# A fused attention, gMLP and expert layer: the key columns of two heads in one product, and the head products in other places

## The reference, cut

```python
q = (c_q @ w_uq).reshape(b, s, 8, 64 + 32)      # c_q: 256 wide, normalised; 32 columns get rope
k_nope = (c_kv @ w_uk).reshape(b, s, 8, 64)     # c_kv: 128 wide, normalised
v = (c_kv @ w_uv).reshape(b, s, 8, 64)
sc = (q_nope . k_nope + q_rope . k_rope) * 96 ** -0.5
sc = where(key_chunk <= q_chunk, sc, -max)      # chunks of 64 tokens
o = softmax(sc) @ v
```

## Time and profile before

| | |
|---|---|
| median of 3 runs | 1146.53 us (1145.36 to 1147.4) |
| profiled execution, span from first to last instruction | 1149.4 us |
| PE busy | 1098.1 us, 96% |
| DVE, ACT, POOL busy | 727.0, 562.0, 378.4 us |
| attention | about 97 to 265 us of the span |
| mean granted TensorE clock | 0.988 |

### The profile page before, as it was taken

One profiled execution on the slowest core, in us unless ns is written; L12 is line 12 of the kernel. 1 busy time (PEld: TensorE's weight loads), 2 busy tenths in 40 slices (PEclk: granted clock), 3 DMA queues, 4 the chain that ended last, 5 costly groups with the idle time before them and its releaser, 6 DMA issues.

```text
span 1149.4 us, 16228 instructions
## 1 busy us (share of the span) xinstructions
PE 1098.1 (96%) x5621; PEld 911.5 (79%) x5621; DVE 727.0 (63%) x939; ACT 562.0 (49%) x740; POOL 378.4 (33%) x270
## 2 busy tenths in 40 slices
PE   4999999999999999999999999979999999999986
PEld 4887888878887888888888788867888888877782
DVE  7877788874066621222223555579999988988847
ACT  6236677673164200000003222248888888878833
POOL 1403222224322233232330000115666666644410
PEclk9999999999999999999999999989999999999998
DMA  8010000022103111211203443569999999999737
GB/s 256 11 30 6 12 7 11 3 74 74 37 1 102 38 51 41 55 42 51 55 2 111 133 138 119 201 233 379 381 390 377 371 357 345 346 364 354 289 137 319
DMA packets 108858, 181.08 MB, mean 158 GB/s; under 512 B 32385, under 2 KB 69761, under 8 KB 108801
## 3 DMA queue, kind: packets, MB, share of 16 engines
q1 hardware_dynamic: 98432, 163.51, 41.4%
q0 software_dynamic: 10368, 16.80, 4.0%
HBM read 174.50 MB, written 26.74 MB: 175 GB/s over the span
## 4 chain that ended last, share of the span: by engine, by line
PE 74%; SPq 9%; DVE 8%; DMA 3%; issue 3%; ACT 2%; POOL 0%; POOLq 0%; ACTq 0%; DVEq 0%
PE ps L399 21%; PE ps L401 20%; PE ps L400 20%; SPq L536 6%; PE ps L765 3%; PE ps L727 2%; DMA raw_e<-in_w_exp_up_dram 2%; PE ps L1012 2%; SPq L532 1%; PE ps L941 1%; DVE negm L1524 1%; DVE pt_lo L1557 1%; DVE we_lo L1860 1%; PE ps L1087 1%; DMA yin<-y_dram 1%
## 5 line engine op out<-in xcount | busy, mean ns | idle before, releaser
L1860 DVE TENSOR_TENSOR we_lo<-raw_e,we_hi 128x2048 fp32r<-128x2048 f32 x105 | 239.7, 2284 | 34.9 <-ACT we_hi L1338 34.7
L1338 ACT ACTIVATE we_hi<-raw_e 128x2048 fp32r<-128x2048 f32 x105 | 200.6, 1912 | 16.5 <-DMA raw_e<-in_w_exp_up_dram 8.6
L399 PE MATMUL ps<-ht_hi,w_hi 128*128 128x512 f32 x432 | 170.1, 394 | 0.7 <-DVE ht_lo L1442 0.4
L401 PE MATMUL ps<-ht_hi,w_lo 128*128 128x512 f32 x432 | 168.3, 390 | 0.0
L400 PE MATMUL ps<-ht_lo,w_hi 128*128 128x512 f32 x432 | 168.2, 389 | 0.0
L393 POOL CAST w_hi<-raw 128x1024 fp32r<-128x1024 f32 x35 | 38.3, 1095 | 275.2 <-PE ps L401 202.2
L1686 DVE TENSOR_TENSOR mix<-ps,mix 128x512 f32<-128x512 f32 x16 | 11.0, 690 | 173.6 <-PE ps L401 173.6
L399 PE MATMUL ps<-we_hi,xst_hi 128*128 128x512 f32 x280 | 115.8, 413 | 0.4 <-DVE xst_lo L1864 0.4
L401 PE MATMUL ps<-we_hi,xst_lo 128*128 128x512 f32 x280 | 110.3, 394 | 0.0
L400 PE MATMUL ps<-we_lo,xst_hi 128*128 128x512 f32 x280 | 109.2, 390 | 0.0
L399 PEld LDWEIGHTS ps<-ht_hi,w_hi 128*128 128x128 f32 x432 | 81.3, 188 | 17.7 <-POOL w_lo L394 0.8
(11 more groups left out here) (311 smaller groups left out, 2518.0 us busy)
## 6 DMA issues: line engine op xcount, KB each, us to landing
raw_e<-in_w_exp_gate_dram SPq DMA_DIRECT2D x70, 512.0 KB, 6.6
raw_e<-in_w_exp_up_dram SPq DMA_DIRECT2D x70, 512.0 KB, 16.2
raw_e<-in_w_exp_down_dram SPq DMA_DIRECT2D x70, 512.0 KB, 8.6
raw<-in_w_in_dram SPq DMA_DIRECT2D x27, 512.0 KB, 3.9
yin<-y_dram SPq DMA_DIRECT2D x16, 512.0 KB, 10.0
xin<-in_x_dram SPq DMA_DIRECT2D x8, 512.0 KB, 8.1
xre<-in_x_dram SPq DMA_DIRECT2D x8, 512.0 KB, 5.3
h_dram<-h SPq DMA_DIRECT2D x8, 512.0 KB, 2.9
```

The lines of the kernel that those rows point to most:

```text
L399: pe.matmul(dst, st[0], mv[0], start=first, stop=False)
L401: return pe.matmul(dst, st[1], mv[0], start=False, stop=last)
L1338: act.activation(we_hi[c % 4][:, :], raw_e[c % NS][:, :], ACT.Copy).then_inc(sem("w_hi_ready"), 1)
L1860: dve.tensor_tensor(we_lo[c % NS][:, :], raw_e[c % NS][:, :], we_hi[c % 4][:, :].bitcast(F32), ALU.subtract).then_inc(sem("w_lo_ready"), 1)
```

## The change

Four things change, and waits and counts with them.

1. The key columns of heads 2m and 2m+1 are one stationary operand of 128 columns. Jobs 1 and 3 exist only for even heads (and are issued while an odd head is worked on); each fills 128 rows of bank 7, and ACT and DVE take each half into the `k_hi` and `k_lo` of its head: two copies and two subtractions per job.
2. `spread_sums` transposes to 64 partitions: the stationary operand has 64 columns, not 128.
3. Job 2 moves from the end of n=4 to the end of n=1. ACT's copy of it moves from n=5 to n=2. Job 1 moves from n=1 to n=4 of odd heads: on PE ahead of the transposes, on ACT behind `probs_high(4)` and ahead of `outputs(2h)`, on DVE behind `probs_low(4)` and ahead of `halves_added(2h)`. On ACT the copies of job 3 stand ahead of the exponential of n=7.
4. Even heads load 384 columns of weights, odd ones 256.

```diff
+        def jobs_of(h):
+            return (0, 2) if h % 2 else (0, 2, 1, 3) if h else (0, 1, 2, 3)
...
+        def keys_at(h, c):
+            return 4 * (h // 2) + 2 * c + h % 2 + 1
...
-                    elif j == 1:
-                        pe.wait_ge(sem("q_tmp_ready"), 2 * h + j // 2 + 1)
-                    elif j == 0 or h < 2 and j == 2:
-                        pe.wait_ge(sem("kv_lo_ready"), 2 * h + j // 2)
+                    elif j == 2:
+                        pe.wait_ge(sem("q_tmp_ready"), 2 * h + 1)
+                    elif j == 0 and h % 2:
+                        pe.wait_ge(sem("kv_lo_ready"), keys_at(h, 1))
                     else:
-                        pe.wait_ge(sem("o_ready"), 2 * (h - 1) + j // 3)
+                        pe.wait_ge(sem("o_ready"), 2 * h - (3, 2, 0, 1)[j])
...
-                        mm = mm3(pe, ps[0:NOPE, b, :], (hh[:, 256:320], hl[:, 256:320]),
+                        mm = mm3(pe, ps[:, b, :], (hh[:, 256:384], hl[:, 256:384]),
                                  (c_hi[:, 0, cs], c_lo[:, 0, cs]), True, True)
...
-                        mm = pe.transpose(ps[:, 7, i * P:(i + 1) * P],
-                                          rl[:, 4 * g + i:4 * g + i + 1].to_broadcast([P, P]), ident[:, :])
+                        mm = pe.transpose(ps[0:VH, 7, i * P:(i + 1) * P],
+                                          rl[:, 4 * g + i:4 * g + i + 1].to_broadcast([P, VH]), ident[:, :])
...
+                        if n == 4 and h % 2 and ahead:
+                            job(h + 1, 1)
                         prob_transposes(h, n)
...
-                        if n in (0, 1, 4, 7) and ahead:
-                            job(h + 1, (0, 1, 4, 7).index(n))
+                        if n in (0, 1) and ahead:
+                            job(h + 1, 2 * n)
+                        if n == 7 and h % 2 and ahead:
+                            job(h + 1, 3)
...
-                        act.activation(k_hi[h % 2][0:64, cs], ps[0:64, job_bank(h, j), :], ACT.Copy).then_inc(sem("kv_hi_ready"), 1)
+                        for i in range(2):
+                            act.activation(k_hi[i][0:64, cs], ps[64 * i:64 * i + 64, job_bank(h, j), :], ACT.Copy).then_inc(sem("kv_hi_ready"), 1)
...
                         probs_high(h, n)
+                        if n in (4, 7) and h % 2 and ahead:
+                            job_high(h + 1, {4: 1, 7: 3}[n])
...
-                        if n in (0, 5, 7) and ahead:
-                            job_high(h + 1, {0: 0, 5: 2, 7: 3}[n])
+                        if n in (0, 2) and ahead:
+                            job_high(h + 1, n)
...
-                        dve.wait_ge(sem("kv_hi_ready"), 2 * h + j // 2 + 1)
-                        dve.tensor_tensor(k_lo[h % 2][0:64, cs], ps[0:64, job_bank(h, j), :], k_hi[h % 2][0:64, cs].bitcast(F32), ALU.subtract).then_inc(sem("kv_lo_ready"), 1)
+                        for i in range(2):
+                            dve.wait_ge(sem("kv_hi_ready"), keys_at(h + i, j // 2))
+                            dve.tensor_tensor(k_lo[i][0:64, cs], ps[64 * i:64 * i + 64, job_bank(h, j), :],
+                                              k_hi[i][0:64, cs].bitcast(F32), ALU.subtract).then_inc(sem("kv_lo_ready"), 1)
...
-                    dve.tensor_tensor(o, ps[r:r + VH, 7, :], o, ALU.mult).then_inc(sem("o_ready"), 1)
+                    dve.tensor_tensor(o, ps[0:VH, 7, :], o, ALU.mult).then_inc(sem("o_ready"), 1)
...
                         probs_low(h, n)
+                        if n == 4 and h % 2 and ahead:
+                            job_read(h + 1, 1)
...
-                        if n in (0, 1, 4, 7) and ahead:
-                            job_read(h + 1, (0, 1, 4, 7).index(n))
+                        if n in (0, 1) and ahead:
+                            job_read(h + 1, 2 * n)
+                        if n == 7 and h % 2 and ahead:
+                            job_read(h + 1, 3)
```

More of the change, by code:

```diff
@@ L160, in build @@
         c_lo = at("c_lo", 120, [P, 3, T], F32R)
-        h_raw = at("h_raw", 200, [P, 320], F32)
-        h_hi = [at(f"h_hi{i}", 201.5 + 3 * i, [P, 320], F32R) for i in range(2)]
-        h_lo = [at(f"h_lo{i}", 203 + 3 * i, [P, 320], F32R) for i in range(2)]
+        h_raw = at("h_raw", 200, [P, 384], F32)
+        h_hi = [at(f"h_hi{i}", 201.5 + 3 * i, [P, 384], F32R) for i in range(2)]
+        h_lo = [at(f"h_lo{i}", 203 + 3 * i, [P, 384], F32R) for i in range(2)]
         wv_raw = at("wv_raw", 12, [P, HEADS * VH], F32)
@@ L444, in job_bank, with jobs_through, job_at, head_loads @@
             return 7 if h else (3, 2, 6, 3)[j]
+        def jobs_of(h):
+            return (0, 2) if h % 2 else (0, 2, 1, 3) if h else (0, 1, 2, 3)
+        def jobs_through(h):
+            return sum(len(jobs_of(g)) for g in range(h + 1))
+        def job_at(h, j):
+            return jobs_through(h - 1) + jobs_of(h).index(j) + 1
+        def keys_at(h, c):
+            return 4 * (h // 2) + 2 * c + h % 2 + 1
+        def head_loads(h):
+            return 16 * (7 * (h // 2) + (4, 7)[h % 2])
+        def head_width(h):
+            return 256 if h % 2 else 384
         def v_tiles_after(jj):
@@ L480, in _ @@
                     sp.dma_start(q[:, :, 112:128], w_uq[:, :, c + 64:c + 80]).then_inc(f, 16)
-                    sp.dma_start(h_raw[:, 256:320], a["w_uk"][0][:, h * 64:h * 64 + 64]).then_inc(f, 16)
+                    if h % 2 == 0:
+                        sp.dma_start(h_raw[:, 256:384], a["w_uk"][0][:, h * 64:h * 64 + 128]).then_inc(f, 16)
                     if h == 1 and "U" in on:
@@ L735, in spread_sums @@
                     pe.wait_ge(sem("rl_ready"), g + 1)
[L736 to L739, removed]
+                    if g == 0 or g % 2 and h + 2 < HEADS:
+                        pe.wait_ge(sem("q_tmp_ready"), 2 * (h + g % 2) + 4)
+                    elif g % 2 == 0 and h % 2 and h + 1 < HEADS:
+                        pe.wait_ge(sem("kv_lo_ready"), keys_at(h + 2, 0))
                     else:
                         pe.wait_ge(sem("o_ready"), g)
-                        pe.wait_ge(sem("kv_lo_ready"), 2 * HEADS)
                     for i in range(4):
-                        mm = pe.transpose(ps[:, 7, i * P:(i + 1) * P],
-                                          rl[:, 4 * g + i:4 * g + i + 1].to_broadcast([P, P]), ident[:, :])
+                        mm = pe.transpose(ps[0:VH, 7, i * P:(i + 1) * P],
+                                          rl[:, 4 * g + i:4 * g + i + 1].to_broadcast([P, VH]), ident[:, :])
                     mm.then_inc(sem("sums_spread"), 1)
@@ L1212, in _ @@
                             exponent(s + 2 + 2 * n)
-                        if n == 1 and ahead:
-                            job_high(h + 1, 1)
                         if n == 0 or n == 1:
@@ L1950, in head_split @@
                 def head_split(h):
-                    pool.wait_ge(sem("hraw_full"), 64 * (h + 1))
+                    w = head_width(h)
+                    pool.wait_ge(sem("hraw_full"), head_loads(h))
                     if h >= 2:
-                        pool.wait_ge(sem("job_done"), 4 * (h - 1))
-                    pool_link(pool, pool.tensor_copy(h_hi[h % 2][:, :], h_raw[:, :]))
-                    pool.tensor_tensor(h_lo[h % 2][:, :], h_raw[:, :], h_hi[h % 2][:, :].bitcast(F32),
+                        pool.wait_ge(sem("job_done"), jobs_through(h - 2))
+                    pool_link(pool, pool.tensor_copy(h_hi[h % 2][:, 0:w], h_raw[:, 0:w]))
+                    pool.tensor_tensor(h_lo[h % 2][:, 0:w], h_raw[:, 0:w], h_hi[h % 2][:, 0:w].bitcast(F32),
                                        ALU.subtract).then_inc(sem("hw_split"), 1)
```

8 lines of the change are left out of this document (4 added, 4 removed).

## The result

| | before | after |
|---|---|---|
| median | 1146.97 us (1145.36 to 1148.82, 4 runs) | 1169.01 us (1167.52 to 1173.21, 4 runs) |
| ratio | | 1.0181, 95% interval 1.0159 to 1.0202 |

A forecast was written before the change was run, and what follows sets the result against it. PE, busy 96%, was taken as the bound, at its limit by a hair against DVE's chain. Start 1.2, head 0 -0.25, even heads 3 x -0.44, odd 3 x 3.1, head 7 -0.35: +8.6; clock +1.7; 1157 us, range 1148 to 1164.

The forecast's parts named there:

- the odd heads: Heads 1, 3, 5: +2.5 us at `values` of chunk 3, +0.8 at chunk 7, -0.2 for sums: +3.1 a head.
- the even heads: Heads 2, 4, 6: `values` of chunk 3 0.3 us late, then -0.22, -0.72 and +0.2: -0.44 us a head.
- the narrower transposes: `spread_sums`, 16 groups of four 64-column transposes: 0.22 us less a group, 3.5 us of PE work in all.
- the clock: Attention: of three idles of about 2.7 us, one was counted as bringing the lower clock, +1.7 us.
- the first transposes behind the low part of chunk 8: End of odd heads: low part of chunk 8 ends later, delaying PE's next-head transposes by 0.8 us (bounds 0.5 and 1.1).
- A key job of 0.72 us: Heads 1, 3, 5, 7 lose two key jobs each, three matmuls of 0.24 us: 8 x 0.72 = 5.7 us less.
- the 0.06 us of one matmul: Sums: a 128-moving-column matmul followed after 0.06 us, weights there; taken as basis for 0.22 us a group.
- rival 4: The 64-column transposes save nothing: forecast + 2, 1159 us; counted inside the forecast's 0.66, no chance of its own.
- The 1.9 us from transposes to `values`: Even heads: `values` of chunk 3 starts some 1.9 us after the transposes of chunk 5, idle ended by the addition.
- The start: Ahead of the loop: head 0's two key jobs have two copies and two subtractions each, PE waits for DVE: +1.2 us.
- Head 0: Chunk 3 late by PE's 0.7 us, then 0.72 + 0.22 less: -0.25 us.
- Rival 3: Clock falls in each odd head, plus a stall or two elsewhere: 8.6 + 3 x 1.7, 1160, up to 1164 us; chance 0.08.

The follow-up runs named there:

- e1: Kernel before with only the shorter transposes that spread the sums (stationary operand of 64 columns instead of 128); 1148.68 us, ratio 1.0006.
- e4: Changed kernel plus transposes nobody reads (22 in heads 1, 3, 5, 13 in the others) ahead of `values` of chunk 3; 1163.37 us, ratio 1.0147.
- e8: Kernel before with only the job order changed in every head (job 2 in chunk 1, job 1 in chunk 4 behind `values`), nothing merged; 1152.87 us, ratio 1.0057.
- e3: Changed kernel with ACT's copies of the second keys product behind the exponential of chunk 7 in heads 1, 3, 5; 1177.37 us, ratio 1.0271.
- e5: e2 with the keys' second half copied and subtracted later (chunks 5 and 9) in odd heads, exponential of chunk 7 first; 1163.16 us, ratio 1.0140.
- e9: e7 with the sums of chunk 6 behind the second scores, output product behind the row maximum, in heads 1, 3, 5; 1156.22 us, ratio 1.0074.
- e6: Changed kernel with job 2 back in chunk 4 in heads 0, 2, 4 and 6; 1167.50 us, ratio 1.0174.
- e2: Changed kernel with chunk 4's keys product, copies and subtractions behind `values`, output copy and addition in heads 1, 3, 5; 1161.96 us, ratio 1.0129.
- e7: Changed kernel with the edits of e5 and e6 together; 1160.20 us, ratio 1.0119.

## Why the prediction was off

In short: the waits came where they were forecast, and two steps of the working failed. The first is the structure, 8.6 us forecast and about 14.7 measured: the odd heads (9.3 forecast, 12.3 measured) were laid beside an even head, and in the even heads (-1.3 forecast, +0.4 measured) the narrower transposes counted 3.5 us of work that turned out as 0.5. The second is the clock, 1.7 us forecast: one fall counted, five came in the trace of after, and keeping PE busy gave back 5.6 us (medians) to 7.6 (traces).

**What bounds the kernel: right, but for one head read for all.** Nearly all the lost time is where the prediction put it: `values` of chunk 3 behind the addition of the halves, and the first transposes behind the low part of chunk 8. The reading that counted was the earlier trace rows beside the earlier trace rows, and not the 96% of the earlier trace rows.

**Work taken from PE: half right.** A key job of 0.72 us was right: over chunk 7 of head 4 the lateness against before falls by 0.69 (15.79 to 15.10). The sums were wrong: 3.5 us counted, 0.5 measured (e1). I took the 0.06 us of one matmul for the price of four; that row's own successor has the full stationary operand, and the row shows a matmul whose weights were there already. The Trainium skill ("TensorE: Matmul & The Clock Gate", section "LDWEIGHTS (loading the stationary operand)") would have the load take half the time with 64 columns, and by it the four would take 0.21 us less, an estimate from its figure; the trace of e1 has 0.03 less, with loads of 111 ns instead of 138. The measurement decides. Why 0.11 us each remain is open.

**Even heads: -0.44 forecast, +0.13 measured.** Three terms: 0.6 instead of 0.3 at `values` of chunk 3 (the transposes of chunk 3 are 0.7 late and not 0.48, since the sums ahead of them gave nothing), 0.2 of the sums of chunk 6 not there, and about 0.1 at chunks 7 and 9. So most of this miss is the term of the sums, rival 4. The 1.9 us from transposes to `values` were 2.16, of them 1.64 idle.

**Odd heads: +3.1 forecast, +4.1 measured (e4).** The chain itself was right nearly to the step. Counted from the head's first transposes (180.49 in head 4 of before, 217.29 in head 5 of after), forecast and measured: keys product 12.61 and 12.64, transposes behind it 13.31 and 13.45, end of the subtractions 16.6 and 16.7, end of the addition 17.2 and 17.4, `values` 17.36 and 17.59; an idle of 2.7 and of 2.78. What failed is the head that I laid it beside. I read head 4 "for all", an even one. PE and DVE of before in head 5:

```profile
215.91 0.49 PE L727 MATMUL ps<-ident,prob 128*128 128x128 f32 x3
216.48 0.36 PE L765 MATMUL ps<-pt_hi,v_c 128*128 128x256 f32 x1
```

```profile
215.64 0.69 DVE L1542 TENSOR_TENSOR o_t<-ps,o_t 64x512 f32<-64x512 f32 x1
```

Here PE idles for only 0.09 us: 0.57 from start to start instead of 0.87, since the addition ends at 216.33, just in time. Heads 1 and 3 are the same (0.58 and 0.58). The odd heads of before were 0.3 us faster at this place, so the same chain costs them +2.8, with its 0.23 of lateness +3.0. Ahead of the next head +1.0 and not +0.8; the sums 0 and not -0.2.

**The start: +1.2 forecast, +0.5 in the ledger, +1.7 measured.** The trace of before is a bad yardstick here: it ran at half clock from 81.1 to 87.9 us, those of after and e1 for half as long (windows view, 80 to 90 us: a mean of 0.66, and 0.83 in both others). From the first value row (`ps<-wv_hi,c_hi`) to the transposes of chunk 1 in head 0 PE takes 23.06 us in e1 and 23.05 in e8, whose work there is that of before, and 24.73 to 24.80 in after, e3, e4, e5 and e9, all with the same mean clock; before itself takes 24.69. The 1.7 us are two waits for DVE, where before and e1 have one for POOL; first the start of head 0's scores in before, then the two places in after:

```profile
93.30 0.32 PE L399 MATMUL ps<-k_hi,q_hi 128*128 128x128 f32 x1 [0.86 <-POOL q_lo L1976]
```

```profile
92.79 0.30 PE L399 MATMUL ps<-k_hi,q_hi 128*128 128x128 f32 x1 [1.61 <-DVE k_lo L1548]
98.87 0.47 PE L399 MATMUL ps<-c_hi,h_hi 128*128 128x512 f32 x1 [0.96 <-DVE v_f L1595]
```

That is the mechanism of the prediction, with 0.5 us more. Head 0 then gave nothing back (+0.3, and -0.25 forecast): with job 2 gone from its chunk 4, it too waits for the addition, 1.36 us.

**The clock: the largest single miss.** One stretch counted, 1.7 us. In the profiled execution there were 17.1 us of half clock in attention, and keeping PE busy in the waits took away 7.6 us in that trace and 5.6 in the medians (1169.01 to 1163.37). I knew of three idles of 2.7 us and had one row in which such an idle cost 1.7 us and one in which a longer one did not; from two rows I drew one of three. All three cost, one of them twice, and an idle of 1.65 us too, once of three times. The same kernels show that this is not a fixed price: e3 has idles of the same length (2.78, 1.65, 2.79, 1.65, 2.78, 1.65) at the same places and falls behind the third to sixth of them, not behind the first and second. Over the heads 1 to 6 of all traces the clock fell at or just behind 8 of 9 idles of 2.78 us (after, e3, e6), 4 of 12 of 1.65 (after, e2, e3, e5) and 2 of 6 of 1.40 (e5, e7), and behind none of 1.36 in head 0 and of 1.55 to 1.59 in head 7. The Trainium skill ("TensorE: Matmul & The Clock Gate", section "Why this matters for your kernels") asks to keep idle gaps between bursts of matmuls short; by these traces a gap of 1.65 us was already too long in four cases of twelve. And an idle is not needed: in all eleven traces the half clock begins at 81 to 83 us, where PE had no wait, at or behind the second of two groups of 16 matmuls with one moving column each (1.84 us a group at full clock). The prediction read one row of half clock in the trace of before and left this one out.

**The sum.** Structure, with the start at 1.7: 1.7 + 0.3 + 3 x 0.13 + 3 x 4.1 + 0 = 14.7 instead of 8.6. Clock: 5.6 by the medians, 7.6 in the traces, instead of 1.7. By the medians that makes 20.3 of the 22.0 us. The forecast was 10.3; of the 10 us between it and 20.3, 6.1 are terms of the structure (3.0 in the odd heads, 1.7 in heads 2, 4 and 6, 0.5 at the start, 0.9 in heads 0 and 7, each head with its share of the sums) and 3.9 are the clock. Rival 3 had the mechanism and gave it a chance of 0.08, at 1.7 us for each of three stretches: five were there. With rival 4 also true, the two together should have been the upper end, and the range stopped short of it; even they make 1166 (1164 + 2), below the fastest execution of after (1167.52).

**What stays open.** The medians of the experiments lie 0.8 to 5.9 us further above before than attention's own shift in their traces: e9 has 9.2 against 4.1, e5 16.1 against 10.2, after 22.0 against 21.2. Part is the trace of before, whose span of 1149.4 is high for it (the runs of before beside e9 have a median span of 1145.2): 1.6 us ahead of attention, by the longer half clock, and some 3 behind it. Even with this e9 keeps about 3 us behind attention whose cause no run isolates; the same code there took 882 us in the traces of e1 and e8 and 886 in those of e5 and e9. One wait in it differs from kernel to kernel: in the last stage PE waits for the expert rows `yin` to come back from DRAM, 2.5 to 3.4 us in the three traces without the merge (before, e1, e8) and 3.8 to 4.7 in the eight with it. Why is not shown. Why the clock falls behind one idle of 1.65 us and not behind the next is not settled either, nor which part of the loss the larger weight loads of the even heads have: no run changes them alone.

## What to carry to other kernels

Ask of every instruction that is moved or merged in what it was hidden, and what it hid: six matmuls in chunk 4 of an even head were free, while three more in chunk 1 cost 0.7 us, as much as the three saved in chunk 7 bring. Read one head of each kind before taking one for all. Merging two products into one halves PE's part alone; the copies and subtractions stay, come in pairs at one place, and hold the PSUM bank longer, which moves the wait from engine to engine as it is repaired (e2, e5, e9). When a change opens idles of 1.5 us and more on TensorE at several places, give the fall of the clock a term of its own, with all of them at the upper end of the range, and a filler run like e4 to tell it from the waits.

## What was not expected of the hardware

- Four 64-column transposes of 128 moving columns take 0.44 us from start to next start, four with 128 columns 0.47: the narrower stationary operand is worth 0.03 us, though each load is 27 ns shorter (111 and 138).
- DVE subtracts PSUM rows 64 to 127 into rows 0 to 63 at the same price: two in 1.40 us, 0.67 to 0.69 each; ACT copies them in 0.57 to 0.60 each.
- The granted clock fell to half behind 4 of 12 idles of 1.65 us and stayed full behind one of 9 of 2.78; it also fell in every trace behind matmuls of one moving column, with no idle at all. Work that nobody reads (13 or 22 transposes in each wait) kept it at 1.00 in attention and made the kernel 5.6 us faster.
